# Two of the ten first expert weight tiles issued without the wait for the first block's gathered rows

## The reference

```python
x  = x + gate1 * (merged @ w_out)
h2 = rms_norm(x, norm2_g) * (1.0 + scale2) + shift2
# router: the best of 4 groups, in it the best 2 of 8 experts, for every token
# the (token, expert) pairs are sorted by expert into blocks of 128 rows
def expert_block(args):
    xi, e = args
    return (jax.nn.silu(xi @ w1[e]) * (xi @ w3[e])) @ w2[e]
out = zeros.at[slot_tok].add(yb * slot_w)          # scatter back to the tokens
x = x + gate2 * out
```

## Time and profile before

| | us |
|---|---|
| median of 3 runs | 1513.78 (1513.48 to 1517.85) |
| the profiled execution, its own time | 1512.96 |
| its span | 1511.2 |
| PE busy in the span | 1459.3 (97%) |
| DVE busy | 579.3 |
| ACT busy | 340.1 |
| POOL busy | 108.7 |
| mean granted TensorE clock | 0.994 |

### The profile page before, as it was taken

How to read it: one execution, slowest core, us unless ns; L and a number is a source line. 1 busy time by engine, 2 the same in 40 slices (tenths; PEclk the granted TensorE clock), 3 DMA queues, 4 the chain that set the end, 5 groups by cost and what they waited for, 6 DMA issues and landing times.

```text
span 1511.2 us, 20868 instructions
## 1 busy us (share of the span) xinstructions
PE 1459.3 (97%) x8371; PEld 710.2 (47%) x8371; DVE 579.3 (38%) x1178; ACT 340.1 (23%) x670; POOL 108.7 (7%) x140
## 2 busy tenths in 40 slices
PE   7999999999999999999999999999998899999996
PEld 3534457787876455444444444543332233333332
DVE  4497444646463247322222455751111011111111
ACT  3513322323336333111111122211110011111110
POOL 2000000000000000000000002001111111111111
PEclk9999999999999999999999999999999999999999
DMA  9780200000012110111122832589999999999994
GB/s 360 251 348 1 64 0 1 29 29 29 29 56 56 29 28 14 43 42 42 42 97 83 333 131 93 195 335 367 419 404 417 404 393 394 406 416 404 405 410 145
DMA packets 79993, 292.50 MB, mean 194 GB/s; under 512 B 13376, under 2 KB 42270, under 8 KB 60961
## 3 DMA queue, kind: packets, MB, share of 16 engines
q1 hardware_dynamic: 73346, 274.51, 46.3%
q0 software_dynamic: 6560, 16.77, 4.4%
HBM read 277.47 MB, written 20.09 MB: 197 GB/s over the span
## 4 chain that ended last, share of the span: by engine, by line
PE 81%; DMA 6%; SPq 5%; DVE 5%; issue 1%; ACT 0%; POOL 0%; POOLq 0%; DVEq 0%; ACTq 0%
PE PS L758 76%; DMA R<-in_expert_w 4%; DVE R L1864 3%; DMA HT<-in_expert_w 2%; SPq L366 2%; SPq L515 2%; PE PS L1380 1%; PE PS L914 1%; DVE att_mx L2075 1%; SPq L510 1%; PE PS L1414 1%; DMA R<-in_ada_w 0%; PE PS L1268 0%; PE PS L858 0%; DVE R L1856 0%
## 5 line engine op out<-in xcount | busy, mean ns | idle before, releaser
L758 PE MATMUL PS<-R 128*32 128x512 f32 (+7 forms) x4158 | 804.8, 566 | 20.2 <-DMA R<-in_ada_w 9.3
L758 PEld LDWEIGHTS PS<-R 128*32 128x32 f32 (+4 forms) x4158 | 296.6, 131 | 397.5 <-issue 372.1
L758 PE MATMUL PS<-HT,R 128*32 128x512 f32 (+2 forms) x1200 | 296.4, 593 | 4.6 <-DMA R<-in_expert_w 2.4
L1856 DVE TENSOR_TENSOR R<-R,PS 128x512 f32<-128x512 f32 (+1 forms) x131 | 95.7, 747 | 473.3 <-PE PS L758 473.3
L758 PE MATMUL PS<-R,HT 128*128 128x512 f32 (+1 forms) x672 | 235.4, 506 | 3.7 <-ACT R L1501 1.5
L758 PEld LDWEIGHTS PS<-R,HT 128*128 128x128 f32 x672 | 125.7, 191 | 94.8 <-issue 81.5
L1501 ACT ACTIVATE R<-PS 128x512 f32<-128x512 f32 (+4 forms) x119 | 71.4, 611 | 429.9 <-PE PS L758 290.3
L758 PEld LDWEIGHTS PS<-HT,R 128*32 128x32 f32 (+1 forms) x1200 | 101.7, 131 | 135.9 <-issue 134.8
L758 PE MATMUL PS<-WK,R 128*32 128x512 f32 (+1 forms) x496 | 106.2, 593 | 1.3 <-DMA HT<-in_expert_w 1.3
L1864 DVE SCALAR_TENSOR_TENSOR R<-PS,R,gate 128x1024 f32<-128x1024 f32 (+1 forms) x23 | 28.5, 1237 | 127.9 <-PE PS L758 127.9
L722 POOL DMA_INDIRECT out_rows<-R x36 | 52.3, 1454 | 296.1 <-DVE R L1864 162.0
(11 more groups left out here) (265 smaller groups left out, 880.2 us busy)
## 6 DMA issues: line engine op xcount, KB each, us to landing
R<-in_expert_w SPq DMA_DIRECT2D x42, 2048.0 KB, 25.7
R<-in_expert_w SPq DMA_DIRECT2D x48, 1024.0 KB, 14.2
HT<-in_expert_w SPq DMA_DIRECT2D x11, 2048.0 KB, 23.9
HT<-in_expert_w SPq DMA_DIRECT2D x18, 1024.0 KB, 11.4
R<-in_ada_w SPq DMA_DIRECT2D x16, 1024.0 KB
WK<-in_expert_w SPq DMA_DIRECT2D x7, 2048.0 KB, 24.4
R<-in_w_in SPq DMA_DIRECT2D x24, 512.0 KB, 4.6
R<-in_ada_w SPq DMA_DIRECT2D x16, 512.0 KB
```

The costliest lines, as they stand in the source:

```text
L758: return nc.tensor.matmul(o, l, r, start=a, stop=z)
L1856: return v.tensor_tensor(o, a, b, op)
```

## The change

One wait is taken out of SP's stream, the one on `xg_ld[0]` for the gather of the first block's rows. The two tiles behind it are then issued when their buffers are free. No other instruction is changed, on any engine.

```diff
             store_x(NT - 1, 1)
             e.wait_ge(s["mo_mm"], 2 * NT)
             load_ew(0, 2, FIXED[2])
-            e.wait_ge(xg_ld[0], 16)
             for u in range(2):
                 e.wait_ge(x1_st[u], 16 * NT // 2)
             load_ew(2, 2, FIXED[2])
```

## The result

| | before | after |
|---|---|---|
| median of six runs, us | 1514.65 (1513.48 to 1517.85) | 1521.34 (1520.77 to 1523.76) |
| span of the profiled execution | 1511.2 | 1520.2 |
| TensorE busy | 1459.3 | 1463.8 |

The changed kernel is slower: its ratio to the kernel before is 1.0036, 95% interval 1.0026 to 1.0047, or +5.5 us (3.9 to 7.1); the two medians are 6.7 us apart, inside that interval. The forecast of slower by over 0.3% came out by the ratio itself, though the interval begins at 0.26%, and 1521.34 lies on the forecast time of 1521. Part of that agreement is luck: the forecast added 7.9 us to an execution of 1512.96, and the six runs of before have their median at 1514.65. As a difference, 7.9 us was too much.

What follows compares the result with a forecast made beforehand. TensorE's own work was taken to be four fifths of the chain of waits. Gather 5.3 us plus clock 2.6 us made 7.9 us on 1512.96, giving 1520.9, stated as 1521 us; range 1514.5 to 1525.

Steps and rivals of the forecast that it cites:

- slower by over 0.3%: Whole kernel: time more than about 0.3% above the kernel before, that is over 1518.3 us; chance 0.70.
- SP's issue: SP's stream: R4 tile issued near 968.5 in place of 978.9, WK tile near 969.7, some 10 us sooner.
- The sooner tiles are worth nothing: Blocks 1 and 2: neither waited for weights, and the DMA queue is empty at 1018 anyway, so no gain.
- The gather's landing, +5.3 us: First block: gather lands 9.4 us after issue, at 983.9, transposes begin at 984.25; bounds 0 to +7.5 us.
- starts about 3 us later and then shares: First block's gather behind the two tiles: first packets about 3 us later, then engines shared with the loads.
- The rival of turns: Gather packets each wait for one load packet: gather 2.7 us longer, 1515.7 us; turns or no harm, chance 0.17.
- The clock, +2.6 us: TensorE before the first block: stands 6.2 us, one clock fall makes its work 2.6 us longer; bounds 0 to 3.4.
- 1:1 to the end: From the first block on: its delay reaches the kernel's end in full, since the loads' schedule follows TensorE's.
- No smaller waits for weights: Past 1129: TensorE's waits for weights do not shrink by as much as the first block is late.

Runs made afterwards that it cites:

- Experiment 5: Kernel before with the R4 and WK tiles issued later still, behind the landing of the gathers of blocks 1 and 2; ratio to before 0.9999.
- experiment 8: Kernel before, wait for the gather's landing replaced by a semaphore counted by a POOL memset behind the gather instruction; ratio to before 0.9997.
- experiment 7: The changed kernel as it is, profiled a second time; lag 8.56 us, distance from the gather's issue to the end 541.9 us.
- experiment 2: Kernel before, wait for the gather's landing replaced by a semaphore POOL's queue counts behind the gather; tiles went 0.2 us ahead of it; ratio to before 1.0031.
- experiment 3: Changed kernel with 8 more fill-in products of TensorE before the first block; ratio to the kernel before 1.0021.
- experiment 4: Kernel before, its wait kept, with 10 more fill-in products of TensorE before the first block; ratio to before 1.0021, +3.2 us.

## Why the prediction was right, point by point

- *SP's issue.* Right: the R4 tile 0.1 us behind the R1 tile, the WK tile 3.2 us behind the store of rows.
- *The sooner tiles are worth nothing.* Right. Experiment 5 moves them later at no cost, experiment 8 issues them 3 us sooner (1.4 us behind the start of the gather in place of 4.4) at no gain, and the loads' queue of the changed kernel is as empty as in the earlier trace rows soon after. In its window of 1019 it moves nothing:

```profile
1019.00:1020.00 1.00, 1.00 (x12) 0.26 (x8) 0.60 (x2) 0.00 (x0) 0.00 (x0) 1.00 0.00 0
```

- *The gather's landing, +5.3 us.* The right mechanism, too large: the lag went from 4.45 and 4.10 to 8.66 and 8.56, **+4.1 to +4.6 us**. The term took 9.4 us for the landing, from the gather of the earlier trace rows that ran beside the same two tiles. Measured were 8.5 us (experiment 7), under the shortest of the contended rows. The row taken is nearer to experiment 2, where the loads were issued only just ahead of the gather: 9.1 us. The term also added 0.35 us from landing to transposes; where TensorE waits for the gather alone it is about 0.1 (8.56 - 8.5). That the gather "starts about 3 us later and then shares" came out: 2.6 us later, and 1.4 us for sharing. The rival of turns (landing 6.8 us after issue, 1515.7) is out as a forecast, since it had no term for the late first packet. Its picture of the sharing is right: one load packet for each of the gather's. But that cost 1.4 us and not 2.7.
- *The clock, +2.6 us.* Right that it falls, too large: the fall cost **0.6 to 1.1 us** in one profile and **1.6 to 2.1** in the other (experiment 3). It goes with how long TensorE works at the low clock. In the earlier trace rows that was from 1141.52 to about 1146.9, 5.3 us, half of which is the 2.6. In the first profile of the changed kernel it was from 987.23 to 990.1, 2.9 us, in the second from 984.95 to 989.8, 4.9 us. That no row of before could tell; within the stated bounds of 0 to 3.4, 2.6 was a value for 5.3 us of low clock, and these falls were shorter.
- *1:1 to the end.* It holds within what can be measured: experiment 4 delays the first block by about 4 us and costs 3.2 us (1.7 to 4.7). From the first transposes to the end of the span the kernel before takes 532.3 and 532.5 us and the changed one 533.0 and 533.4; of what was forecast to be unchanged but for the clock, 0.8 us is left, which is less than the scatter of a profile and can't be told from the cost of the clock.
- *No smaller waits for weights.* TensorE's waits for weights from 960 on sum to 14.5 us against 14.0, so nothing was taken up there.

The sum of the measured terms, 4.3 us for the gather and 0.6 to 2.1 for the clock, is 4.9 to 6.4 us and lies within the interval of 3.9 to 7.1 us; the forecast sum of 7.9 lies above it.

## What to carry to other kernels

A wait that looks like a needless dependency between two DMAs may be what keeps the first one's way clear: before taking it out, look at what else is on the critical path and goes through the same engines at that time. A small DMA that others wait for should be at the engines before large ones are issued; 1.4 us of distance was enough here, and waiting for its landing was not needed. The tiles that were loaded sooner were worth nothing here, since the queue ran empty soon after in any case: look for such an empty moment before counting on a gain.

## What the runs showed of the hardware

The first gather issued by POOL landed in 4.0 to 4.2 us where the DMA engines were idle (both profiles of the kernel before, experiment 5), and in 8.3 to 9.1 where two tiles of SP were issued ahead of it (experiments 3, 7 and 2). The larger part is the wait for its first packet: 0.6 us behind the end of POOL's instruction at 975.74 in the kernel before, 3.2 us behind it in the changed kernel, 3.1 with one tile ahead. The smaller is the sharing, packet for packet (46, 45 and 44 of the gather to 45, 46 and 46 of the loads), which cost about 1.4 us.

Loads issued 1.4 us after the gather's start left it nearly as fast as alone (lag 4.73 us), loads issued 0.2 us before it made it as slow (9.17) as loads that had been running for 7 us (8.66).

In experiment 2 a semaphore that POOL's own queue counts behind the gather had been counted before the gather began (SP issued at 975.34, the gather started at 975.54). In experiment 8 one that an operation behind the gather counts came after the gather's instruction (977.02 + 0.11, SP issued at 977.15).
